# Stick-breaking attention: suffix products from pairs of float32r parts instead of float32 operands

## The reference, cut to what matters

```python
def stick_breaking(q, k, v, bias, q_pos, k_pos):
    z = jnp.einsum('bqhd,bkhd->bhqk', q, k) * (HEAD_DIM ** -0.5) + bias
    mask = k_pos[None, :] < q_pos[:, None]
    log_keep = jnp.where(mask, jax.nn.log_sigmoid(-z), 0.0)
    later = lax.cumsum(log_keep, axis=3, reverse=True) - log_keep
    w = jnp.where(mask, jnp.exp(jax.nn.log_sigmoid(z) + later), 0.0)
    return jnp.einsum('bhqk,bkhd->bqhd', w, v)
```

## Time and profile before

| quantity | value |
|---|---|
| median of three runs | 3793.74 us |
| profiled execution | 3794.87 us |
| its span on the core | 3793.2 us |
| TensorE busy, share of the span | 3348.2 us, 88% |
| VectorE busy | 1883.2 us, 50% |
| ScalarE busy | 1518.0 us, 40% |
| GpSimd busy | 1074.2 us, 28% |
| first unit to last unit of the attention | 885 to 1855 us |

### The profile page before, as it was taken

One profiled execution on the slowest core, in us unless ns is written; L12 is line 12 of the kernel. 1 busy time (PEld: TensorE's weight loads), 2 busy tenths in 40 slices (PEclk: granted clock), 3 DMA queues, 4 the chain that ended last, 5 costly groups with the idle time before them and its releaser, 6 DMA issues. The chain is left out here.

```text
span 3793.2 us, 48151 instructions
## 1 busy us (share of the span) xinstructions
PE 3348.2 (88%) x14713; PEld 2293.3 (60%) x14713; DVE 1883.2 (50%) x2584; ACT 1518.0 (40%) x2479; POOL 1074.2 (28%) x929
## 2 busy tenths in 40 slices
PE   6666767667999999999779979999999999999998
PEld 4444555533444444444268857778777877777777
DVE  5888797894332233323145545534553455345542
ACT  3222423205665666656333334423442344223332
POOL 5999698633333333333101110000000000000000
PEclk8778888778999999999879989999999999999999
DMA  7999798714446654564444543343334333433333
GB/s 248 314 307 300 245 303 263 106 34 121 145 148 174 177 156 146 163 192 148 156 168 138 150 120 97 92 149 104 92 93 151 100 96 104 139 115 124 123 112 113
DMA packets 527291, 590.68 MB, mean 156 GB/s; under 512 B 82457, under 2 KB 338521, under 8 KB 526507
## 3 DMA queue, kind: packets, MB, share of 16 engines
q1 hardware_dynamic: 491704, 562.35, 49.0%
q10 hardware_dynamic: 35224, 25.46, 2.1%
q0 software_dynamic: 176, 0.56, 0.1%
HBM read 525.77 MB, written 61.38 MB: 155 GB/s over the span
## 5 line engine op out<-in xcount | busy, mean ns | idle before, releaser
L2322 PE MATMUL ffn_bank<-ffn_xh,ffn_wh 128*128 128x512 f32 x1408 | 557.9, 396 | 18.6 <-DVE ffn_wl L2536 18.2
L353 POOL TENSOR_TENSOR project_Kr<-project_Kr,project_q_wide 128x1024 f32<-128x1024 f32 x205 | 545.9, 2696 | 65.4 <-DMA project_Kr<-in_cache_k_dram 65.1
L2322 PE MATMUL ffn_bank<-ffn_xl,ffn_wh 128*128 128x512 f32 x1408 | 549.5, 390 | 0.0
L2322 PE MATMUL ffn_bank<-ffn_xh,ffn_wl 128*128 128x512 f32 x1408 | 548.8, 390 | 0.0
L1525 DVE SCALAR_TENSOR_TENSOR att_X<-att_X,att_bank 128x512 f32<-128x512 f32 (+2 forms) x320 | 192.9, 610 | 521.1 <-ACT att_X L1430 520.0
L1385 POOL TENSOR_TENSOR att_S<-att_S,att_X 128x512 f32<-128x512 f32 (+3 forms) x256 | 283.0, 1106 | 339.8 <-PE att_bank L1625 317.9
L2279 POOL TENSOR_TENSOR ffn_st<-ffn_st,kept_eps 128x1 f32<-128x1 f32 x16 | 4.9, 307 | 1216.1 <-ACT ffn_stage L2520 1119.9
L535 DVE TENSOR_REDUCE project_zs<-project_Kr 128x16 f32<-128x1024 f32 x256 | 303.1, 1216 | 84.9 <-POOL project_Kr L353 83.0
L2322 PEld LDWEIGHTS ffn_bank<-ffn_xh,ffn_wh 128*128 128x128 f32 x1408 | 264.9, 188 | 95.2 <-DVE ffn_wl L2536 31.0
L2322 PEld LDWEIGHTS ffn_bank<-ffn_xh,ffn_wl 128*128 128x128 f32 x1408 | 264.9, 188 | 56.4
L2322 PEld LDWEIGHTS ffn_bank<-ffn_xl,ffn_wh 128*128 128x128 f32 x1408 | 265.2, 188 | 52.4
(11 more groups left out here) (360 smaller groups left out, 6116.2 us busy)
## 6 DMA issues: line engine op xcount, KB each, us to landing
project_Kr<-in_cache_k_dram SPq DMA_DIRECT2D x512, 256.0 KB, 4.0
att_Vr<-in_cache_v_dram SPq DMA_DIRECT2D x512, 256.0 KB, 3.4
ffn_wdf<-in_w_down_dram SPq DMA_DIRECT2D x108, 512.0 KB, 3.4
ffn_stage<-in_w_gate_dram SPq DMA_DIRECT2D x89, 512.0 KB, 3.9
ffn_stage<-in_w_up_dram SPq DMA_DIRECT2D x88, 512.0 KB, 4.5
project_w<-in_w_in_dram SPq DMA_DIRECT2D x40, 512.0 KB, 6.0
project_xt<-in_x_prompt_dram SPq DMA_DIRECT2D x16, 512.0 KB
att_qf<-qT_dram SPq DMA_DIRECT2D x64, 128.0 KB, 3.6
```

The lines of the kernel that those rows point to most:

```text
L353: pool.tensor_tensor(Kr[:, k % KR], Kr[:, k % KR], q_wide[:, b % 2, None, :].to_broadcast([P, 2, AW]), ALU.mult).then_inc(k_pool, 1)
L2322: mm = pe.matmul(bank[:, first + f % 2, :], w[:, j, k, :], x[:, k, :], start=(k == 0 and n == 0), stop=(k == KD - 1 and n == 2))
```

## The change

The two suffix products take float32r operands. Each float32 operand is replaced by a pair: the operand rounded to float32r, and the rest (operand minus rounded), rounded in turn. One float32 product becomes two float32r products with the same weights, which accumulate in the bank.

- `X`: VectorE rounds it into `Xh` directly behind the softplus and subtracts it into `Xl` (both in its step s for unit s - 1).
- `S`: ScalarE rounds the sum into `Sh` (`round_carry`, in its step s for unit s - 2, between ln and the exp of the weights). The rest `Sl` is subtracted by VectorE or by GpSimd: of the 36 units that make a sum, every second one by each (`rest_on_pool`). VectorE does it in step s for unit s - 3, between the rounding and the rest of `X`; GpSimd does it for unit u - 1 behind the sum of unit u.
- `S` has three slots instead of two, and a slot is free when its rounding and its rest are done; GpSimd no longer waits for `logw_ready`. ScalarE waits for `logw_ready` before it writes a slot of `Sh`.
- TensorE multiplies `S` first and `X` after it. `negtri`, `negones`, the identity and the mask are copied to float32r once, by ScalarE, at the start of the stage; the mask's product is float32r too.

```diff
-        NX, NW, NZ = 4, 4, 5
+        NX, NW, NZ, NSUM = 4, 4, 5, 3
...
-        S = m.sb("S", [P, 2, CH])
+        Xh, Xl = m.sb("Xh", [P, NX, CH], F32R), m.sb("Xl", [P, NX, CH], F32R)
+        S = m.sb("S", [P, NSUM, CH])
+        Sh, Sl = m.sb("Sh", [P, NSUM, CH], F32R), m.sb("Sl", [P, NSUM, CH], F32R)
...
+                def rest(b, u):
+                    o = cols(u)
+                    pool.wait_ge(sh_ready, b * CARRIES[-1] + CARRIES[u])
+                    pool.tensor_tensor(Sl[:, u % NSUM, o:], S[:, u % NSUM, o:], Sh[:, u % NSUM, o:].bitcast(F32), ALU.subtract
+                                       ).then_inc(sl_pool, 1)
...
-                        pool.wait_ge(logw_ready, b * NU + u)
+                        if u >= NSUM:
+                            v = max(v for v in range(u - NSUM + 1) if carries(v))
+                            pool.wait_ge(sh_ready, b * CARRIES[-1] + CARRIES[v])
...
                             pool.tensor_tensor(new[:, r:], old[:, r:], x[:, r:], ALU.add).then_inc(s_part, 1)
+                        if u and carries(u - 1) and rest_on_pool(u - 1):
+                            rest(b, u - 1)
...
+                act.wait_ge(consts, 8)
+                for out, src in ((tri_r, negtri), (ones_r, negones), (ident_r, ident), (fill_r, fillm)):
+                    act.activation(out[:], src[:], ACT.Copy).then_inc(rounded, 1)
...
+                def round_carry(b, u):
+                    o = cols(u)
+                    act.wait_ge(s_part, b * SUMS[-1] + SUMS[u])
+                    if not (isinstance(b, int) and b == 0 and u < NSUM):
+                        act.wait_ge(logw_ready, b * NU + u - NSUM + 2)
+                    act.activation(Sh[:, u % NSUM, o:], S[:, u % NSUM, o:], ACT.Copy).then_inc(sh_ready, 1)
...
+                        r, u = behind(b, s, 2, first, rest)
+                        if u is not None and carries(u):
+                            round_carry(r, u)
...
                             stt(x, x, LN_TOP, z, ALU.min, ALU.max).then_inc(sp_ready, 1)
+                            if not first or u >= NX:
+                                dve.wait_ge(logw_ready, units_to(r, u, NX, first))
+                            dve.wait_ge(sp_ready, r * NU + u + 1)
+                            dve.tensor_copy(Xh[:, u % NX, cols(u):], x).then_inc(xh_ready, 1)
...
+                            tt(Xl[:, u % NX, o:], X[:, u % NX, o:], Xh[:, u % NX, o:].bitcast(F32), ALU.subtract).then_inc(xl_ready, 1)
...
+                            tt(Sl[:, u % NSUM, o:], S[:, u % NSUM, o:], Sh[:, u % NSUM, o:].bitcast(F32), ALU.subtract).then_inc(sl_dve, 1)
...
-                            pe.wait_ge(sp_ready, r * NU + u + 1)
-                            last = pe.matmul(bank[:, u % NZ, o:], negtri[:], X[:, u % NX, o:], start=False, stop=True,
-                                             skip_group_check=True)
                             o2 = o + P if diag(u) else o
                             if o2 < CH:
-                                pe.wait_ge(s_part, r * SUMS[-1] + SUMS[u - 1])
-                                last = pe.matmul(bank[:, u % NZ, o2:], negones[:], S[:, (u - 1) % 2, o2:], start=False, stop=True,
+                                if rest_on_pool(u - 1):
+                                    pe.wait_ge(sl_pool, r * POOL_RESTS[-1] + POOL_RESTS[u - 1])
+                                else:
+                                    pe.wait_ge(sl_dve, r * DVE_RESTS[-1] + DVE_RESTS[u - 1])
+                                for part in (Sh, Sl):
+                                    pe.matmul(bank[:, u % NZ, o2:], ones_r[:], part[:, (u - 1) % NSUM, o2:], start=False, stop=False,
+                                              skip_group_check=True)
+                            pe.wait_ge(xl_ready, r * NU + u + 1)
+                            for part in (Xh, Xl):
+                                last = pe.matmul(bank[:, u % NZ, o:], tri_r[:], part[:, u % NX, o:], start=False, stop=part is Xl,
                                                  skip_group_check=True)
```

More of the change, by code:

```diff
@@ L1186, in stage_attention @@
     SUMS = [sum(steps(v) for v in range(u + 1)) for u in range(NU)]
+    carries = lambda u: U[u][1] != 0
+    CARRIES = [sum(carries(v) for v in range(u + 1)) for u in range(NU)]
+    rest_on_pool = lambda u: CARRIES[u] % 2 == 0
+    POOL_RESTS = [sum(carries(v) and rest_on_pool(v) for v in range(u + 1)) for u in range(NU)]
+    DVE_RESTS = [CARRIES[u] - POOL_RESTS[u] for u in range(NU)]
     with ExitStack() as ctx:
@@ L1208, in stage_attention @@
         zero, fillm = m.sb("zero", [P, P]), m.sb("fillm", [P, P])
+        tri_r, ones_r, ident_r, fill_r = (m.sb(n, [P, P], F32R) for n in ("tri_r", "ones_r", "ident_r", "fill_r"))
         Vr = m.sb("Vr", [P, VSLOTS, PP, AW])
@@ L1425, in round_ @@
                             if not first or s >= NX:
-                                act.wait_ge(logw_ready, units_to(b, s, NX, first))
+                                act.wait_ge(xl_ready, units_to(b, s, NX, first))
                                 act.wait_ge(s_part, b * SUMS[-1] + (SUMS[s - NX] if s >= NX else SUMS[NU + s - NX] - SUMS[-1]))
@@ L1530, in round_ @@
                             softplus()
+                        rest_of_carry()
+                        if s == 0 or not rest:
+                            rest_of_softplus()
                         r, u = behind(b, s, LAG + 2, first, rest)
@@ L1571, in _ @@
                 pe.wait_ge(consts, 8)
+                pe.wait_ge(rounded, 4)
                 def samples_v(b, n):
@@ L1611, in round_ @@
                                 if q == 0 and diag(s):
-                                    pe.matmul(bank[:, s % NZ, o:o + P], ident[:], fillm[:], start=False, stop=False,
+                                    pe.matmul(bank[:, s % NZ, o:o + P], ident_r[:], fill_r[:], start=False, stop=False,
                                               skip_group_check=True)
```

29 lines of the change are left out of this document (26 added, 3 removed).

## The result

The changed kernel takes 3943.78 us (median of four runs, 3941.28 to 3949.65) against 3796.64 us for the kernel before on the same chip: a ratio of 1.0387, 95% interval 1.0362 to 1.0413. The prediction, 3770 us, had the wrong sign, and its range (3670 to 3870) does not hold the result.

The account below looks back on a forecast made before the run. Prediction: turns of VectorE and GpSimd at SBUF replace TensorE as the bound; 3.21 us per full unit, 117.5 per head, attention 946 against 970 us, 24 off the median gives 3770 us, range 3670 to 3870.

Parts of the forecast that it names:

- What bounds the kernel before: Attention: TensorE sets the pace, busy 120.75 of 124 us per head; the change would cut it to 93 us.
- The ScalarE term: Attention, ScalarE: 36 roundings per head add 20 us, raising its work from 76 to 96 us per head.
- VectorE and GpSimd share something at SBUF: Attention: their two-input passes and casts take turns; holds GpSimd 1.13, VectorE's subtraction 0.55, its rounding 0.28 us.
- rival 2: VectorE's cast to float32r needs no turn and runs beside GpSimd's sum: 2.99 us per unit, 3728 us; chance 0.10.
- One pair of full units: Attention: two full units, one with S's rest on GpSimd, one on VectorE, take 6.42 us, 3.21 per unit.
- One head: Attention: full, j = 0 and narrow units sum to 106 us; with VectorE's other work and TensorE delays, 117.5 per head.
- The sum: Attention: 8 x 117.5 plus 5 and 1 gives 946 us against 970, so 3770 us for the whole kernel.
- Rival 3: GpSimd takes two turns in a row before VectorE: 3.65 us per unit on average, 3854 us; chance 0.22.
- break-even of 3.34 per full unit: Attention: the change loses from 120.5 us per head on, that is 3.34 us per full unit, 0.13 above the forecast.
- Rival 4: TensorE's clock partly drops to 1.2 GHz in the attention: 115 us more, 3885 us; chance 0.08.
- the sign named for it: Attention: TensorE's granted clock (PEclk) falling below 0.95 would show the forecast wrong.
- Rival 1: GpSimd's turns hide beside VectorE's softplus and ScalarE bounds: 100 us per head, 3630 us; chance 0.15.

Follow-up runs that it names:

- Run 9: The changed kernel with GpSimd's rest of S done one unit later (unit u - 2 instead of u - 1), all work still done: 3893.64 us, ratio 1.0254.
- run 7: The changed kernel with all parts still made, but TensorE multiplying float32 X and S as before, with added waits for TensorE: 3944.58 us, ratio 1.0375.

## Why the prediction was wrong, point by point

- **What bounds the kernel before**, and what TensorE gains: right at the full clock. The product of 512 columns costs 0.23 us as predicted, and with half the work made the full units fell to 2.7 us. But TensorE was busy 111.5 us per head, not 93, because part of the head ran at the lower level: in the stretch granted 0.67 two such products start at 1418.94 and 1419.37, 0.43 apart. The ScalarE term was right too: the roundings take 19.8 us per head (predicted 20), its busy time 92.9 (96).
- **VectorE and GpSimd share something at SBUF**: right, and so were the prices: 1.13 (measured 1.12 to 1.15), 0.55 (0.55 to 0.59), 0.28 for the cast (0.27 and 0.28). The Trainium skill (SBUF — State Buffer, "Who interferes with whom") speaks of an exclusive lock on the shared port pair; the rows of both kernels agree, and the softplus, which reads z from PSUM, kept its 0.67 beside both of GpSimd's operations.
- **The cast is not a two-port pass (rival 2)**: wrong. It has 0.43 where nothing holds it and is held behind GpSimd.
- **One pair of full units: this step failed.** I wrote "the first with the rest of S on GpSimd, the second on VectorE". The change defers them differently: behind the sum of unit u GpSimd does the rest of u - 1, in the step of the softplus of u VectorE does the rest of u - 2. They take opposite parities, so both fall beside the same u. The rows of the two queues stood in the text ahead of the prediction, but I laid them side by side by the unit that a rest belongs to, not by the one in which it is done. The pair is 7.34 us in place of 6.42, (3.70 - 3.21) x 20 = 9.8 us per head, 78 in all. Run 9 removes 7.9 of the 9.8 by timing alone.
- **One head: this step failed too, and by more.** The other 20 units were sized at 53.3 us and took 65.8, 12.5 more per head, 100 in all. I took 70% of VectorE's once-per-head 13.7 us as added and gave splits no cost on ScalarE. The loss is mostly behind chunk 2: the four full units of chunk 1 took 22.2 us, where four at 3.21 are 12.8, and the eight units after them 25.8, where my terms (2 x 2.3 and 2 x 4.8) give 14.2; the 10 and the 1.5 that I had added cover 11.5 of these 21 us. At 1412 to 1428 us VectorE is busy 15.56 of 16 us; the runs with the splits apart show that a split costs its place 3.7 us, in part as a wait for ScalarE. Every variant has this part at 58 to 80 us, above the 55.7 of the kernel before, whose TensorE hid it. The lower clock has a share of it in the narrow units (run 7), a small one by the rows shown. How the rest divides between VectorE's load and the loop over ScalarE and TensorE in the narrow units is open: no run parts them.
- **The sum**: 8 x (9.8 + 12.5) = 178, and 3770 + 178 = 3948, against 3944 measured. The phase, which the runs show, is the smaller part of it: with it mended (run 9, 3894) the kernel is still slower than the one before.
- **Rival 3** gave 3.65 per unit (its own two, 3.95 and 3.4, average 3.68); 3.66 to 3.70 came, but not by its mechanism: in the timelines read, GpSimd never had two turns in a row while VectorE waited. Its break-even of 3.34 per full unit was useful: run 9, with 3.30, is still slower than before only because of the other 20 units. **Rival 4** (clock): the sign named for it came, 0.87 in the attention against 0.95, but it is not the cause in the full units, which are as long at 1.00 with TensorE 78% busy as at 0.86; in the narrow ones it costs a little. **Rival 1** (the sharing hides) is excluded for this order, though with all rests on GpSimd most of each rest does hide.

## What to carry to other kernels

Where two engines share a port, write their queues side by side by the step in which each instruction runs, with its lag, before pricing the steady state: here one unit of lag was worth 0.4 us per unit, and 4.51 and 2.83 by turns is how it shows. Put GpSimd's passes under VectorE passes that need no turn, or leave them on VectorE: a two-input pass costs it 0.60 us alone and 1.15 when it waits for GpSimd to do the same. And price once-per-head work in full as soon as the engine that does it becomes the bound, with its wait for the other engine that has a part in it.

## What the runs showed of the hardware that was not expected

- Handing a two-input pass to GpSimd can cost VectorE more than doing it: the full unit took 3.01 us with GpSimd idle and 3.70 with its help.
- Loosening a wait made a kernel slower (3744 to 3769 us) with no work added.
- The order of turns isn't fixed. In the steady unit with all rests on VectorE the sum goes ahead of VectorE's cast (the cast's record is 1.53 us, both subtractions behind it have 0.68), in the change it goes behind it. That the order alone changes a unit's length is not shown: this unit has 3.44 us, and the expectation, with the cast ahead, came to 3.4.

```profile
1241.63 1.53 DVE L1570 CAST att_Xh<-att_X 128x512 fp32r<-128x512 f32 x1
1243.09 0.68 DVE L1586 TENSOR_TENSOR att_Sl<-att_S,att_Sh 128x512 fp32r<-128x512 f32 x1
1243.69 0.68 DVE L1578 TENSOR_TENSOR att_Xl<-att_X,att_Xh 128x512 fp32r<-128x512 f32 x1
```
